# Four small moves in a two-block transformer kernel: one exponential, one logarithm, one sum of squares, one product

## The reference, cut to what matters

```python
# first block, mixer
h = rms_norm(x, norm_mix_g)
aq, ak, av, hq, hf, hi, hg, ga, gh = split_combined(h @ w_in)
# hgrn2_recurrence, in chunks of 32 tokens
f = lower_bound + (1 - lower_bound) * sigmoid(hf);  k = 1 - f
b = cumsum(log(f), axis=chunk)
q_dec = silu(hq) * exp(b);  k_inv = k * exp(-b)
decay = exp(b_last);        ds = (k * exp(b_last - b))^T @ v
o = o_intra + o_inter
o = rms_norm(o, hgrn_norm_g) * silu(hg)          # mean over 128, + 1e-6, power -1/2
merged = sigmoid(ga) * (y_attn @ w_attn_proj) + sigmoid(gh) * (y_hgrn @ w_hgrn_proj)
x = x + merged @ w_out
# every norm over the model width
y = x * (mean(x * x) + 1e-6) ** -0.5 * g
```

## Time and profile before

| | |
|---|---|
| median of 3 timed runs | 1443.85 us (1443.55 to 1445.56) |
| the profiled execution | 1443.56 us, its span 1441.8 us |
| granted TensorE clock, mean | 0.999 |
| TensorE busy | 1422.6 us (99%) |
| VectorE, ScalarE, GpSimd busy | 967.4, 738.5, 212.7 us |
| DMA | 245 MB, 170 GB/s on average |
| the chain that ended last | TensorE 77%, issue 14%, VectorE 4%, ScalarE 4%, GpSimd 1% |

### The profile page before, as it was taken

The page is one execution under the profiler, slowest core; times in us unless marked ns, Lnnn a source line. Parts: engine busy times, 40 slices in busy tenths (PEclk is TensorE's granted clock), DMA queues, the critical chain, the costliest instruction groups (busy, mean ns, idle before and its releaser), DMA issues.

```text
span 1441.8 us, 25221 instructions
## 1 busy us (share of the span) xinstructions
PE 1422.6 (99%) x10281; PEld 1290.2 (89%) x10281; DVE 967.4 (67%) x1752; ACT 738.5 (51%) x1066; POOL 212.7 (15%) x122
## 2 busy tenths in 40 slices
PE   8999999999999999999999999999999999999997
PEld 7989989999999999998777778888899788899986
DVE  5565674693944777778888876655577864677754
ACT  5674654545454444444444445544567754655543
POOL 5000000488883000000000000000114100000000
PEclk9999999999999999999999999999999999999999
DMA  6433456455555545445545466555543453455552
GB/s 241 142 132 125 138 157 216 141 186 180 187 180 182 170 162 174 164 164 173 174 164 174 164 222 245 181 185 188 175 147 118 159 177 112 154 188 185 181 190 103
DMA packets 67219, 245.07 MB, mean 170 GB/s; under 512 B 7456, under 2 KB 7712, under 8 KB 66848
## 3 DMA queue, kind: packets, MB, share of 16 engines
q1 hardware_dynamic: 66960, 243.19, 50.5%
q10 hardware_dynamic: 144, 0.26, 0.0%
HBM read 242.37 MB, written 1.05 MB: 169 GB/s over the span
## 4 chain that ended last, share of the span: by engine, by line
PE 77%; issue 14%; DVE 4%; ACT 4%; POOL 1%; DMA 0%; POOLq 0%; SPq 0%; DVEq 0%; ACTq 0%
PE bank L433 76%; ACT A L1154 2%; DVE wlo L1712 1%; ACT whi L1154 1%; PE bank L442 1%; DVE A L1712 1%; ACT L1154 1%; DVE A L1708 0%; DVE xres L1712 0%; DMA xres<-in_x 0%; POOL wlo L2555 0%; ACT hTh L1154 0%; DVE small L2361 0%; DVE small L1712 0%; POOL small L2561 0%
## 5 line engine op out<-in xcount | busy, mean ns | idle before, releaser
L1712 DVE TENSOR_TENSOR wlo<-raw,whi 128x1024 fp32r<-128x1024 f32 (+1 forms) x375 | 458.1, 1223 | 334.3 <-ACT whi L1154 333.9
L1154 ACT ACTIVATE whi<-raw 128x1024 fp32r<-128x1024 f32 (+1 forms) x450 | 472.9, 1053 | 401.3 <-PE bank L433 401.3
L433 PE MATMUL bank<-hTh,whi 128*128 128x256 f32 x1944 | 555.5, 286 | 2.0 <-DVE wlo L1712 1.3
L433 PE MATMUL bank<-hTl,whi 128*128 128x256 f32 x1944 | 548.6, 282 | 0.0
L433 PE MATMUL bank<-hTh,wlo 128*128 128x256 f32 x1944 | 548.0, 282 | 0.0
L433 PEld LDWEIGHTS bank<-hTh,whi 128*128 128x128 f32 x1944 | 367.0, 189 | 5.9 <-DVE wlo L1712 2.1
L433 PEld LDWEIGHTS bank<-hTh,wlo 128*128 128x128 f32 x1944 | 366.0, 188 | 0.0
L433 PEld LDWEIGHTS bank<-hTl,whi 128*128 128x128 f32 x1944 | 365.5, 188 | 0.3 <-issue 0.2
L433 PE MATMUL bank<-whi,hTh 128*128 128x512 f32 (+2 forms) x552 | 218.4, 396 | 0.2
L433 PE MATMUL bank<-wlo,hTh 128*128 128x512 f32 (+2 forms) x552 | 215.0, 390 | 0.0
L433 PE MATMUL bank<-whi,hTl 128*128 128x512 f32 (+2 forms) x552 | 214.9, 389 | 0.0
(11 more groups left out here) (178 smaller groups left out, 1391.8 us busy)
## 6 DMA issues: line engine op xcount, KB each, us to landing
raw<-in_u SPq DMA_DIRECT2D x128, 512.0 KB, 3.3
raw<-in_v SPq DMA_DIRECT2D x128, 512.0 KB, 3.3
raw<-in_w_up SPq DMA_DIRECT2D x44, 512.0 KB, 3.3
raw<-in_w_down SPq DMA_DIRECT2D x22, 512.0 KB, 3.2
raw<-in_w_in_t SPq DMA_DIRECT2D x17, 512.0 KB, 3.4
raw<-in_w_in_g SPq DMA_DIRECT2D x16, 512.0 KB, 3.3
raw<-in_w_out SPq DMA_DIRECT2D x16, 512.0 KB, 4.0
raw<-in_w_pq SPq DMA_DIRECT2D x16, 512.0 KB, 3.5
```

The source lines that it names most:

```text
L433: return e.matmul(o, l, r, start=st, stop=sp_, skip_group_check=True)
L1154: return e.activation(o, i, func, **kw)
L1712: return e.tensor_tensor(o, a, b, op)
```

## The change

On ScalarE the yield between the two exponentials and the decay moves up, between the first and the second exponential: `h_kinv` is issued behind the next high part. The logarithms of the recurrence's norm, and with them all that follows in ScalarE's `hgrn`, are issued a unit later; on VectorE a yield is added behind the multiplication with the norm, ahead of the low part of y_hgrn. In the three norms with quarters, ScalarE adds columns 4 and 5 with an Identity that has one as its bias, once its own last sum has been written, and signals `n_part`; VectorE adds column 8, 1e-6 and column 9 in one operation. At the end GpSimd's product comes ahead of both powers.

```diff
@@ act_program: part_squares, after the last square
+                e.wait_ge(s["n_sq"], 4 * {0: 1, 3: 6, 4: 7}[r] + 2)
+                act(small[:, 9:10], small[:, 4:5], ACT.Identity, bias=small[:, 5:6]).then_inc(s["n_part"], 1)
@@ act_program: hgrn
                 act(eb, h_b, ACT.Exp).then_inc(s["hg_act"], 1)
+                yield
                 act(h_kinv, h_b, ACT.Exp, scale=-1.0).then_inc(s["hg_act"], 1)
-                yield
                 act(decay.unsqueeze(2), bl, ACT.Exp).then_inc(s["hg_act"], 1)
@@ dve_program: part_add_and_sum
-                st = small[:, 4:8]
-                e.wait_ge(s["n_sq"], 4 * r + 2)
-                own(ts(small[:, 9:10], st[:, 0:1], st[:, 1:2], EPS, ALU.add, ALU.add))
-                again()
-                tt(st[:, 3:4], small[:, 8:9], small[:, 9:10], ALU.add).then_inc(s["n_sum"], 1)
+                e.wait_ge(s["n_part"], PARTS[at])
+                stt(small[:, 7:8], small[:, 8:9], EPS, small[:, 9:10], ALU.add, ALU.add).then_inc(s["n_sum"], 1)
@@ pool_program: end
-            rstd(7, (0,))
             e.wait_ge(s_gf2, 16)
             e.wait_ge(s["r_add"], 19)
             e.tensor_tensor(xg[:, D:D + 512], xres[:, D:D + 512], gfin2[:, 0:512], ALU.mult).then_inc(s["f_xd"], 1)
-            rstd(7, (1,))
+            rstd(7)
```

More of the change, by code:

```diff
@@ L155 @@
 ff_a ff_c ff_g ff_h ff_lo
-own_act own_dve own_pool zeros x_sq hi_half lo_half lo_first f_xg f_xd f_act hd_mask
+own_act own_dve own_pool zeros x_sq hi_half lo_half lo_first f_xg f_xd f_act n_part hd_mask
 """.split()
```

## The result

The changed kernel takes 1446.93 us (median of 20 runs, 1445.07 to 1448.39) against 1443.94 us of the kernel before beside it (20 runs, 1443.29 to 1445.63). The ratio is 1.0019, with a 95% interval of 1.0013 to 1.0025: 3 us slower, and outside the forecast's range of 1444.4 to 1446.2. Its profiled execution took 1446.58 us with a span of 1444.8, that is 3.02 more than before.

What follows compares the result with a forecast made beforehand. TensorE, busy 1422.6 of 1441.8 us, was taken as the bound; -0.62 + 1.58 + 0.46 - 0.10 = +1.32 us took the profiled 1443.56 to 1444.9, a timed median of 1445.2, range 1444.4 to 1446.2.

Steps and rivals of the forecast that it cites:

- rival D: In the new gap before w_ap 2 the clock falls, TensorE runs at half rate: 1446.9 to 1448.5 us; chance 0.08.
- Part 1: At 104 us in w_in_g: h_kinv's exponential behind the high part removes TensorE's whole stall, -0.62 us.
- Rival C: At 104 us: moving h_kinv's exponential gives nothing, something else holds that high part; 1445.8 us, chance 0.08.
- Part 2: Before w_ap: the later logarithm removes the 1.92 us stall but opens one of 3.53 before w_ap 2, +1.58 us.
- Rival B: Before w_ap: the later logarithm pays, the 1.92 us stall goes and no new one comes; 1441.7 us, chance 0.12.
- Part 3: Norms behind w_out and w_xo: the Identity on ScalarE delays the scalings by 0.23 us each, +0.46 us.
- Part 4: Behind the last matmul: GpSimd's earlier product speeds block 1's power, delays the first two output transfers; -0.10 us.

Runs made afterwards that it cites:

- b_log_only: The kernel before with only the later logarithm, behind the copy of unit 15: 1447.52 us, ratio 1.0020.
- b_exp_only: The kernel before with only h_kinv's exponential moved behind the high part: 1443.17 us, ratio 0.9994.
- b_ahead: The kernel before with h_kinv's exponential moved and the logarithm behind w_ap 1's high part but ahead of unit 15's copy: 1441.18 us, ratio 0.9976.
- a_filler: The changed kernel with twelve filler matmuls on zeros behind w_ap 1, in the gap: 1445.47 us, ratio 1.0005 to the kernel before.

## Why the prediction was wrong

The step that failed is the clock: the sum has no term for it, and the weighing of rival D gave it a chance of 0.08. The forecast said that "today's gap of 1.76 between matmuls leaves the clock alone". That was read from one execution. In 40 of 85 the same gap brings the slower level, and a stop nearly twice as long brings a slower level in 19 of 20 runs of the changed kernel. The second reason, that the new gap is shorter than the idle time ahead of the fall at the end (3.7 us), does not hold either: in b_log_only the clock fell 2.0 us after the last matmul had ended (166.18 to 168.18), and in the changed kernel 1.4 us after work had started again.

The price of the rival was nearly right: 1.65 for a stretch like the one at the program's start, 1.48 measured, and a stretch twice as long, which it also named, was seen. That its 1446.9 meets the measured 1446.93 is in part luck. The sum without the clock was 0.43 too low (below), the price 0.17 too high, and the forecast started from a median of 1443.85 over three runs, 0.21 above the lower level. The spread of the three times given for before (1443.55 to 1445.56) already held both levels, and the forecast did not ask why runs of one kernel differ by 2 us.

The Trainium skill (TensorE: Matmul & The Clock Gate, Part 1) calls the throttled state the default, which activity releases. The traces agree: the clock fell behind a stop of 3.45 us and came back while TensorE worked on. The forecast named the rule as speaking for rival D and did not let it move the chance.

Point by point, forecast and measured:

- Part 1: -0.62, measured -0.70. The whole stall goes; what was missed is that the first matmul behind a wait is slower (0.38 in place of 0.28), and that goes too. Rival C is refuted by b_exp_only.
- Part 2: +1.58 without the clock, measured +1.58 for the start of w_ap 2, and 0.11 for its slower first matmul, which the forecast left out. The hole itself was 3.61 (forecast 3.53): a unit without a wait takes 2.88, not 2.95, so that w_ap 1 ended sooner. The copy of unit 15 stands in front of the logarithm and the chain of the earlier trace rows follows whole. Rival B is refuted; b_ahead, where the logarithm is in the same later step but ahead of the copy, shows that the copy was what hurt.
- Part 3: +0.46, measured +0.66. The mechanism was right and the Identity was mis-sized: it started 0.03 behind the accumulator read, as forecast, but takes 0.29, and lets the next one start 0.20 behind its own start, not 0.11. The model was a small operation of another kind (128x8).
- Part 4: -0.10, measured +0.10. Block 1's power came 0.70 earlier (forecast 0.8). The first output scaling, and with it the first transfer, came 1.0 later (forecast 0.7 for the transfers): the product started 0.74 behind the last matmul (forecast 0.66), and block 0's power behind it took 0.75, where it had taken 0.55.
- Clock: nothing, measured +1.48 in the profiled execution.

Without the fall the sum would have been -0.70 + 1.58 + 0.11 + 0.66 + 0.10 = +1.75 (forecast +1.32), which on the lower level of the kernel before gives 1445.4; the one run of the changed kernel with a mean clock of 0.999 took 1445.07, and a_filler 1445.47, beside the forecast of 1445.2.

## What to carry to other kernels

When TensorE bounds a kernel, a hole in its row can have two prices, the time that it stands and the time at the lower clock behind it, and the second can be as large as the first (here 1.48 or 2.34 beside 1.58). Before a gap is called harmless for the clock, look at the spread of the runs beside the one profile: two levels for one kernel can mean that the profile shows only one of the cases. When a step on an in-order engine is moved later, look first at which wait it is moved behind. Part 2 alone, with the logarithm behind the copy, lost 0.20%; with the logarithm just ahead of the copy, together with part 1, the kernel gained 0.24%, and part 1 is only 0.7 us of that.

## What the runs showed of the hardware

- A stop of TensorE of 1.9 us was followed by a spell at half clock in 40 of 85 executions of the kernel before, judged by the level of their times, and one of 3.6 us in 30 of 31, judged likewise (the two kernels that have it). The fall came 1.4 us after TensorE had restarted in one trace and 1.5 us before it did in another; the spells took 3.41 and 6.83 us, and matmuls of 128x256 stood 0.213 us apart in them, where 0.120 is usual.
- Twelve or six matmuls on zeros in the gap, which leave 0.84 and 0.45 us of it, kept all 22 runs on the lower level, and no fall shows in either trace before the program's end.
- The first matmul behind a wait for a low part has its successor 0.22 us behind it, where 0.12 is usual, so that each such wait costs 0.1 us more than its length.
- An Identity over one element for each partition with its addend read from memory takes 0.29 us on ScalarE and holds the next instruction back by 0.20; a 128x8 operation holds it by 0.11.
- A power of one element for each partition on GpSimd took 0.55 alone (1437.26 in the trace before), 0.55 beside VectorE's add out of PSUM (1434.66), 0.75 beside its sum of squares, and 0.99 beside its scaling of xres with two inputs of SBUF (1040.01), and the sum of squares took 0.98 beside GpSimd's product against 0.42. The Trainium skill (SBUF — State Buffer, Who interferes with whom) says of this pair that one holds the other off; the traces agree, in both directions.
